# Zero products ahead of the first tokens, two more PSUM banks for turned tiles, and GpSimd making parts of three weight tiles

## What is computed

```python
x = layer_norm(x, ln_in_g, ln_in_b)      # 2048 prompt + 32 sample tokens, 1024 channels
proj = x @ w_in                          # 1024 -> 9 * 256 columns
xa, ga, xb, gb, gc, q, k, v, xp = jnp.split(proj, 9, axis=-1)
...
x = layer_norm(ALPHA * x + mix @ w_out, ln1_g, ln1_b)
x = layer_norm(ALPHA * x + sq_relu_mlp(x, w_ff1, w_ff2), ln2_g, ln2_b)
```

## Time and profile before

| | us |
|---|---|
| median of 3 runs | 2443.58 (2443.28 to 2446.14) |
| span of the profiled execution | 2440.8 |
| what lies around the span (the median less the span) | 2.8 |
| TensorE busy in the span | 2406.7 (99%) |
| VectorE busy | 1585.0 (65%) |
| ScalarE busy | 1286.6 (53%) |
| GpSimd busy | 243.0 (10%) |

### The profile page before, as it was taken

One profiled execution on the slowest core, in us unless ns is written; L12 is line 12 of the kernel. 1 busy time (PEld: TensorE's weight loads), 2 busy tenths in 40 slices (PEclk: granted clock), 3 DMA queues, 4 the chain that ended last, 5 costly groups with the idle time before them and its releaser, 6 DMA issues.

```text
span 2440.8 us, 36724 instructions
## 1 busy us (share of the span) xinstructions
PE 2406.7 (99%) x13263; PEld 2331.5 (96%) x13263; DVE 1585.0 (65%) x2233; ACT 1286.6 (53%) x1982; POOL 243.0 (10%) x527
## 2 busy tenths in 40 slices
PE   7999999999999999999999999999999999999998
PEld 7999999999999999999999999999999999999998
DVE  7635662656777787777788777757655665764335
ACT  5466523555655745656555565554455555444432
POOL 0012320200001100011100111000122130000000
PEclk9999999999999999999999999999999999999999
DMA  8434554534444434444443443333566674343332
GB/s 257 153 108 143 159 174 138 184 111 130 162 134 139 142 110 144 150 129 144 128 124 117 137 141 124 125 122 114 182 187 187 209 234 134 120 136 117 112 118 83
DMA packets 141526, 351.64 MB, mean 144 GB/s; under 512 B 20625, under 2 KB 64146, under 8 KB 141218
## 3 DMA queue, kind: packets, MB, share of 16 engines
q1 hardware_dynamic: 128994, 312.88, 40.6%
q0 software_dynamic: 12352, 36.42, 4.7%
HBM read 300.11 MB, written 49.12 MB: 143 GB/s over the span
## 4 chain that ended last, share of the span: by engine, by line
PE 95%; DVE 2%; ACT 2%; DMA 1%; issue 1%; SPq 0%; DVEq 0%; ACTq 0%
PE PS L1136 22%; PE PS L1138 22%; PE PS L1137 22%; PE PS L874 5%; PE PS L872 5%; PE PS L873 5%; PE PS L942 2%; PE PS L964 1%; PE PS L932 1%; PE PS L963 1%; PE PS L1026 1%; PE PS L933 1%; PE PS L1056 1%; PE PS L1014 1%; PE PS L912 1%
## 5 line engine op out<-in xcount | busy, mean ns | idle before, releaser
L1440 ACT ACTIVATE w_hi_lo<-w_raw 128x1024 fp32r<-128x1024 f32 x240 | 252.7, 1053 | 283.5 <-PE PS L1138 277.3
L1136 PE MATMUL PS<-a_hi,w_hi_lo 128*128 128x416 f32 x1080 | 385.1, 357 | 1.3 <-DVE w_hi_lo L1995 1.3
L1138 PE MATMUL PS<-a_hi,w_hi_lo 128*128 128x416 f32 x1080 | 379.3, 351 | 0.0
L1137 PE MATMUL PS<-a_lo,w_hi_lo 128*128 128x416 f32 x1080 | 378.6, 351 | 0.0
L1995 DVE TENSOR_TENSOR w_hi_lo<-w_raw,w_hi_lo 128x1024 fp32r<-128x1024 f32 x240 | 292.6, 1219 | 58.1 <-ACT w_hi_lo L1440 55.9
L1136 PE MATMUL PS<-h_hi,w_hi_lo 128*128 128x416 f32 x824 | 294.6, 358 | 0.0
L1138 PE MATMUL PS<-h_hi,w_hi_lo 128*128 128x416 f32 x824 | 290.2, 352 | 0.0
L1137 PE MATMUL PS<-h_lo,w_hi_lo 128*128 128x416 f32 x824 | 289.4, 351 | 0.0
L2022 DVE TENSOR_TENSOR h_lo<-h_full,h_hi 128x416 fp32r<-128x416 f32 x160 | 94.6, 592 | 222.9 <-ACT h_hi L1455 222.8
L1136 PEld LDWEIGHTS PS<-a_hi,w_hi_lo 128*128 128x128 f32 x1080 | 203.0, 188 | 4.1 <-DVE w_hi_lo L1995 1.7
L1137 PEld LDWEIGHTS PS<-a_lo,w_hi_lo 128*128 128x128 f32 x1080 | 203.5, 188 | 2.1
(11 more groups left out here) (336 smaller groups left out, 5203.8 us busy)
## 6 DMA issues: line engine op xcount, KB each, us to landing
w_raw<-w_all SPq DMA_DIRECT2D x380, 512.0 KB, 3.5
proj_scratch<-stage SPq DMA_DIRECT2D x70, 208.0 KB, 1.9
k_rows<-kv_out SPq DMA_DIRECT2D x80, 128.0 KB, 4.0
v_hi_lo<-v_scratch SPq DMA_DIRECT2D x40, 256.0 KB, 4.1
x_scratch<-x_full SPq DMA_DIRECT2D x20, 416.0 KB, 2.9
x_residual<-x_scratch SPq DMA_DIRECT2D x5, 1664.0 KB, 7.6
pages<-ck SPq DMA_DIRECT2D x64, 128.0 KB, 2.2
pages<-ck POOLq DMA_DIRECT2D x64, 128.0 KB, 2.5
```

Of the source, the lines that this page charges most:

```text
L1136: pe.matmul(out, w_h, mh_[:, k, :], start=(g == 0), stop=False)
L1137: pe.matmul(out, w_h, ml_[:, k, :], start=False, stop=False)
L1138: ins = pe.matmul(out, w_l, mh_[:, k, :], start=False, stop=(g == KT - 1))
L1440: act.activation(halves(w_hi(n)), raw_halves(n), ACT.Copy).then_inc(s_wh, 1)
```

## The change

1. TensorE gets ten products of zeros (`keep_busy`), 128 x 128 by 128 x 384 in fp32 into PSUM bank 7, ahead of the transposes of block 0. They are released in pieces: three when the first row has landed, two at the third row, two at the fourth, two when the variance is made, one when the shift is made.
2. The turned tiles 4 to 7 of block 0 go to banks 2 to 5 instead of 4 to 7; only tiles 6 and 7 still wait, each for one scaled tile.
3. GpSimd makes both parts of weight tile 1 (a copy that rounds, then the subtraction) and the low parts of tiles 2 and 3. ScalarE loses `split_hi(1)`, VectorE `split_lo(2)` and `split_lo(3)`. `split_lo(0)` moves on VectorE from ahead of `block_back(0)` to behind its first scaled tile.

```diff
+        def back_bank(b, k):
+            return k - 2 if b == 0 and k >= 4 else 4 + k % 4
+        def back_free(b, k):
+            if b == 0:
+                return 1 if k >= 6 else 0
+            return 4 if b == 1 and k < 4 else b * 4 + (k - 4) // 2 + 1
...
-                if k >= 4 or b:
-                    pe.wait_ge(s_xfd if k % 2 else s_xfa, b * 4 + (k - 4) // 2 + 1)
+                if back_free(b, k):
+                    pe.wait_ge(s_xfd if k % 2 else s_xfa, back_free(b, k))
...
+            def keep_busy(count):
+                for _ in range(count):
+                    pe.matmul(PS[:, 7, 0:3 * P], gsel[:, 0, 0, :], gsel[:, 0, :, :].rearrange("p n c -> p (n c)"), start=True, stop=True)
+            pe.wait_ge(s_mzero, 1)
+            pe.wait_ge(s_xr0[0], 32)
+            keep_busy(3)
+            pe.wait_ge(s_xr0[2], 32)
+            keep_busy(2)
+            pe.wait_ge(s_xr0[3], 32)
+            keep_busy(2)
+            pe.wait_ge(s_ve, 1)
+            keep_busy(2)
+            pe.wait_ge(s_nmr, 1)
+            keep_busy(1)
...
             split_hi(0)
-            split_hi(1)
...
+                        if b == 0 and k == 1:
+                            split_lo(0)
...
             block_nmr(0)
-            split_lo(0)
             dve.wait_ge(s_const, 32)
             block_back(0, range(KT))
-            dve.wait_ge(s_wl, 2)
-            split_lo(2)
             block_var(1)
             block_nmr(1)
-            split_lo(3)
...
+            pool.wait_ge(s_raw[1], 16)
+            pool.tensor_copy(halves(wp_hi(1)), raw_halves(1)).then_inc(s_hi1, 1)
+            pool.wait_ge(s_hi1, 1)
+            pool.tensor_tensor(halves(wp_lo(1)), raw_halves(1), halves(wp_hi(1)).bitcast(F32), ALU.subtract).then_inc(s_lo1, 1)
+            pool.wait_ge(s_lo1, 1)
+            pool.wait_ge(s_wh, 1)
+            pool.sem_inc(s_wh, 1)
             pool.wait_ge(s_wl, 1)
-            pool.wait_ge(s_wh, 2)
-            pool.tensor_tensor(halves(wp_lo(1)), raw_halves(1), halves(wp_hi(1)).bitcast(F32), ALU.subtract).then_inc(s_wl, 1)
+            pool.sem_inc(s_wl, 1)
+            for p in (2, 3):
+                pool.wait_ge(s_wh, p + 1)
+                pool.tensor_tensor(halves(wp_lo(p)), raw_halves(p), halves(wp_hi(p)).bitcast(F32), ALU.subtract).then_inc(s_wl, 1)
```

More of the change, by code:

```diff
@@ L441, in build @@
         s_wh, s_wl = sem("w_hi_made"), sem("w_lo_made")
+        s_hi1, s_lo1 = sem("second_w_hi_made"), sem("second_w_lo_made")
         s_xin, s_t1st = [sem("xin_in_a"), sem("xin_in_b")], [sem(f"x1_stored{n}") for n in range(4)]
@@ L846, in turn_back @@
                     pe.wait_ge(s_natv, 3 * (b + 1))
-                if k >= 4 or b:
-                    pe.wait_ge(s_xfd if k % 2 else s_xfa, b * 4 + (k - 4) // 2 + 1)
+                if back_free(b, k):
+                    pe.wait_ge(s_xfd if k % 2 else s_xfa, back_free(b, k))
                 for j in range(NR):
-                    ins = pe.transpose(PS[:, 4 + k % 4, j * ROW:(j + 1) * ROW], x_rows(b)[0:ROW, j, k * P:(k + 1) * P],
+                    ins = pe.transpose(PS[:, back_bank(b, k), j * ROW:(j + 1) * ROW], x_rows(b)[0:ROW, j, k * P:(k + 1) * P],
                                        ident[0:ROW, 0:ROW])
@@ L1300, in block_back @@
                         place_free(act, s_xl, b, k)
-                        act.activation(x_full(b, k), PS[:, 4 + k % 4, 0:BLK], ACT.Identity, bias=ln_gb[:, 1, k:k + 1],
+                        act.activation(x_full(b, k), PS[:, back_bank(b, k), 0:BLK], ACT.Identity, bias=ln_gb[:, 1, k:k + 1],
                                        scale=ln_gb[:, 0, k:k + 1]).then_inc(s_xfa, 1)
@@ L1738, in block_back @@
                         place_free(dve, s_xh, b, k)
-                        dve.tensor_scalar(x_full(b, k), PS[:, 4 + k % 4, 0:BLK], ln_gb[:, 0, k:k + 1], ln_gb[:, 1, k:k + 1],
+                        dve.tensor_scalar(x_full(b, k), PS[:, back_bank(b, k), 0:BLK], ln_gb[:, 0, k:k + 1], ln_gb[:, 1, k:k + 1],
                                           ALU.mult, ALU.add).then_inc(s_xfd, 1)
+                        if b == 0 and k == 1:
+                            split_lo(0)
                         for d in (k - 1, k):
@@ L1765, in op @@
                 own.sync()
+            dve.wait_ge(s_wl, 4)
             split_lo(4)
```

## The result

| | kernel before | changed kernel |
|---|---|---|
| median, 21 runs each | 2443.86 us (2442.32 to 2446.14) | 2447.34 us (2445.16 to 2451.88) |
| span of the profiled execution | 2440.8 | 2445.6 |

The ratio is 1.0015, with a 95% interval of 1.0009 to 1.0022: the change costs 3.5 us. That is more than nothing and less than the 0.2% (4.9 us) set as the bound for "slower". The profiled execution took 2447.34 us in all, so 1.7 us lie around its span; the difference of the spans, 4.8 us, is larger than that of the medians because single executions differ by more than a microsecond.

A forecast was written before the change was run, and what follows sets the result against it. TensorE, busy for 99% of the span, was taken to bound the kernel. The projection's 4.7 us plus the port's 1.9 minus 0.2 made 6.4 us later: 2450.0 us, from 2443.6; range 2441.5 to 2455.

The forecast's parts named there:

- E: Mark: end of TensorE's two-tile projection of block 0, at 32.69 before; forecast 37.4, 4.7 us later.
- the configuration pair: GpSimd, block 0: configuration records between the copy and tile 1's subtraction; cost between nothing and 16.5 us, taken as 8.2.
- The copy: GpSimd's rounding copy of weight tile 1 in block 0: taken as 2.4 us, from 14.4 to 16.8.
- The port: GpSimd's subtraction for tile 3 holds up VectorE's shift of block 1 through shared SBUF access: 1.9 us.
- SyncE's queue ... Free: Load of raw tile 3 waits behind tile 1's late low part; tile used 0.6 us after E; no cost.
- T: Mark: TensorE's first transpose of block 1, at 37.25 before; forecast E + 6.45 instead of E + 4.56.
- (a): The forecast itself: slower through the configuration pair, 2446 to 2455, with 1.4 us for a low clock at the projection; chance 0.62.
- U: Mark: TensorE's first transpose of block 2, at 54.23 before; beyond it the change was to alter nothing.
- Rival (b): Configuration pair free, port not: E 30.4, shift held up until 34.5, T 36.85; 2443.0, no change; chance 0.22.
- Rival (c): Everything works: pair free, copy in a gap of VectorE, nothing held up; T 33.6, total 2439.7; chance 0.08.
- Rival (d): TensorE's clock stays low through the zero products: takes 2.3 us from Rival (c); within 0.2% either way; no chance given.
- The zero products: TensorE, ahead of block 0's transposes: over by 14.4, cost nothing, could give 1.4 us through faster transposes and matmuls.

The follow-up runs named there:

- a: Changed kernel with the low part of weight tile 3 back on VectorE, behind block 1's normalisation: 2444.36 us, ratio 1.0006.
- d: Kernel before with only the zero products and the two more banks, nothing moved to GpSimd: 2444.54 us, ratio 1.0006.
- b: Changed kernel with five more zero products just ahead of block 1's first transpose: 2447.68 us, ratio 1.0018.
- h: Changed kernel with GpSimd's copy waiting for block 0's normalising, plus five more zero products ahead of block 1's first transpose: 2444.76 us, ratio 1.0005.
- e: Changed kernel with GpSimd's copy also waiting until VectorE has normalised block 0: 2448.00 us, ratio 1.0021.
- c: Changed kernel without its ten zero products: 2447.49 us, ratio 1.0017.
- f: Changed kernel with tile 3's low part on VectorE, GpSimd's copy after block 0's normalising, ScalarE's block 1 root and normalising ahead of tile 3's high part: 2443.28 us.
- g: Kernel f without the ten zero products: 2442.06 us, ratio 0.9994; measured again 2442.55 us, ratio 0.9995.
- k: Kernel g with the low part of weight tile 1 on VectorE too: 2442.08 us, ratio 0.9995.
- the changed kernel again: The changed kernel measured once more, unchanged, giving its second profile: 2447.20 us, ratio 1.0017.

## Why the prediction was right and where it failed

The direction (later) and the range were right. The size was 3.5 us, not 6.4, so the change stayed inside 0.2%, to which I had given 0.38, and not outside, to which I had given 0.56. The way there was another than I forecast, and that the total came out near is luck: of the 6.4 us, the 4.7 ahead of E did not happen (E came 2.8 us sooner), and two terms that I had put at nothing, or not at all, took their place. By the signs that I had named myself the forecast mechanism is wrong twice over: the subtraction follows the copy within a microsecond, and E comes before 32.69 with tile 1 early.

**The step that failed is the configuration pair**: "I take the middle, 8.2". It costs at most 0.08 us: the subtraction starts 0.08 us after the copy ends, and the pair's two records there last 1 ns each. I had taken the middle between nothing and the 16.5 us that happened to precede the next instruction in the kernel before. That upper bound was the length of a wait for something else and bore on the pair in no way; the pair's own 8 to 11 ns was the nearer row. The Trainium skill (GPSIMD Engine Reference, Instruction dispatch) tells of a first call of about 6 us; no run here shows it for this subtraction. With the pair falls all that hung on it: TensorE did not stop after three matmuls, and E is 29.90, not 37.4. The copy was over-priced as well, 2.4 us taken, 1.16 and 1.39 measured here and 1.04 in the changed kernel's second profile; at the memset's rate, my 0.9 us was near.

**The port was right, and its size too.** The forecast was 1.9 us for the shift of block 1, and it is 2.06 - 0.16 = 1.9. The faster form with one tensor input, for which no row was to be had, is held up as well: 4.76 us instead of 1.99 in a. The low part of tile 0 took 2.66 us instead of 1.22, beside GpSimd's subtraction at 16.72. The statistics are not held up: eight in 4.84 us, with a whole subtraction of GpSimd at 27.10 beside them, and 4.84 in d with none. The Trainium skill (SBUF — State Buffer, Who interferes with whom) says that whoever issues first keeps the shared ports for its whole instruction; the traces agree, down to a shift of 16 bytes a partition, and in the other order too: in the changed kernel's first profile the copy, issued at 15.25 while VectorE normalised until 15.74, took 1.39 us instead of 1.04.

**"SyncE's queue ... Free" was wrong.** I took the load of raw tile 3 to hang on the low part of tile 1. It hangs on the last scaled tile of block 0, through the stores ahead of it in the queue, and did not move with E: the high part of tile 3, due at E + 0.6, began at E + 2.28. This put T at E + 7.93 and not at E + 6.45: 1.7 us for the tile, less 0.2 for details.

**The clock behind T was missing.** No step asked what TensorE's clock does if E comes early and T doesn't; in (a) I had priced it at the projection (1.4 us), where it did not fall. It fell at T, where the wait was 3.24 us, and cost 3.1 in that trace. That the slow stretch behind T is the clock is seen in the granted clock (0.50) and in b and h, where a filled wait brings the transposes back to 1.62 us and T to U back to 17.0. What it costs the median is less sure: h against e, which differ only in the filled wait, gives 3.2 us, of which the traces place 0.9 ahead of U, and b against the changed kernel, the same edit, gives nothing.

**Rival (b) had the mechanism**: pair free, port not, E 30.4 (29.90), the shift held up until 34.5 (35.71), T 36.85 (37.83). It gave 2443.0; with the two terms that it lacked, 1.0 us at T and 3.3 from T to U (20.07 instead of 16.78), it is 2447.3. **Rival (c)** assumed that an early E makes T early. d shows that this fails even without the subtractions handed to GpSimd: T 36.48, not 33.6, because VectorE's statistics did not start at 25.0, but at 28.00. Even in the changed kernel, where the low part of tile 2 is off VectorE, they start at 26.61: 1.3 us sooner than before, where I had counted 2.9. **Rival (d)** did not occur in the changed kernel: block 0's transposes behind the zero products took 3.04 us.

**The zero products** were over at 15.24 (forecast 14.4) and free, as said. The 2.0 us that they save in the transposes do not reach T: c has the median of the changed kernel.

So the gain was there and went: E is 2.8 us sooner, 1.9 go to the port, 1.7 to the late tile (less the 0.2), which leaves T 0.6 later, and in this trace the clock takes 3.1 more. f, which mends the first two and so the third, has T 1.4 us sooner than the kernel before, with no wait. What is shown is that the subtraction for tile 3 on GpSimd is the main loss (a) and that the loss is gone when it, the copy and the order on ScalarE are put right (f, g, k). What stays open: how much of the median is the clock behind T, why the traces differ by up to 3.3 us behind U, and why b's median is 3.2 us above its profiled execution. Port meetings at block 0 that differ by execution were seen (normalising 1.99 to 4.76 us), but e, which takes them away, kept a wide range of its own; so that this is the cause is argued, not shown.

## What to carry to other kernels

Time won on the bounding engine counts only at the next point where it waits for others: follow the chain that makes the next block's operands (here the statistics, the root, the shift, and the queue of the next weight tile) and move that first, or the gain becomes an idle stretch, behind which the clock can be low on top. A long GpSimd instruction on SBUF belongs beside work that it doesn't hold up (statistics, reads of PSUM), never beside a tiny instruction on the path. An unknown cost is not the middle between nothing and a number that merely was not contradicted: an upper bound must come from something that the cost could have produced.

## What the runs showed of the hardware that was not expected

- A wait of 2.16 us (d) or 2.23 us (e) at T was followed by the 1.2 GHz level (transposes 3.00 and 2.84 us), as were those of 3.24, 3.40 and 4.51 us. After waits of 0.50, 0.54, 0.94 and 1.12 us the level stayed at 2.4 GHz (1.62 us each). At the projection of block 0 idle times of 1.82 us (changed kernel) and 1.71 (d) left it up, 2.11 left it up in h and not in e and f. An idle time alone does not tell.
- A second low stretch, 1700 us later: in most traces the clock falls once more near 1745 us, where TensorE goes over to matmuls of 32 columns (32 of them from 1745.23 in e) after an idle 0.3 us. The windows of TensorE in e:

```profile
1744.00:1748.00 4.00, 3.70 (x31) 1.00 0.72 246
1748.00:1752.00 4.00, 4.00 (x17) 0.55 0.33 115
1752.00:1756.00 4.00, 4.00 (x15) 0.60 0.77 247
```

  In h it is 0.84 and 0.73 for 1744 to 1752 and 1.00 behind; in the changed kernel's first profile and in b it is 1.00 throughout. From U to the end the traces take 2386.6 to 2389.9 us, though the program there is the same; the four longest (a, e, k and the changed kernel again, 2388.4 to 2389.9) all have the long form of this stretch. It is not the whole difference: c has the long form at 2387.9, the kernel before has a short one (0.69 and 0.89) and is the shortest of all, and the changed kernel's first profile has none and takes 1.1 us more. What makes it fall in some executions was not tried.
- The profile's granted clock reads 1.00 from the start of the span until its first change: in the kernel before it is 1.00 for 22 to 25 us, where the starts are 0.35 us apart. At the start of a program the distance of the starts is the surer reading.
- Where GpSimd issues a copy and a subtraction back to back, the order of issue decides. In a VectorE's last normalising instruction begins at 15.0, behind the subtraction (14.92), and takes 2.85 us instead of 0.81. In the changed kernel's second profile it begins at 15.0 too, ahead of the subtraction (16.15): it ends at 16.61, and the subtraction takes 2.72 us instead of 2.38. VectorE, then GpSimd:

```profile
13.84 2.77 DVE L1757 TENSOR_SCALAR rows_a<-rows_a,rstd,nmr 104x1024 f32<-104x1024 f32 x3
```

```profile
15.03 1.04 POOL L2442 CAST w_hi_lo<-w_raw 128x1024 fp32r<-128x1024 f32 x1 [14.39 <-DMA w_raw<-w_all]
16.15 2.72 POOL L2444 TENSOR_TENSOR w_hi_lo<-w_raw,w_hi_lo 128x1024 fp32r<-128x1024 f32 x1
```

- Moving a 128 x 1024 tile with rounding takes GpSimd 1.04 us undisturbed, the subtraction of the same shape 2.4, twice VectorE's 1.22.
